# Reordering VectorE and ScalarE around the second projection and attention, the norm behind them and a gated mixer's first chunk

## The reference, cut to what matters

```python
for i in range(2):
    h = h + 0.5 * swiglu(rmsnorm(h, norm_g[i, 0]), ffn_w_in[i, 0], ffn_w_out[i, 0])
    hn = rmsnorm(h, norm_g[i, 1])
    h = h + (mixer_a(hn, ...) if i == 0 else mixer_b(hn, ...))
    h = h + 0.5 * swiglu(rmsnorm(h, norm_g[i, 2]), ffn_w_in[i, 1], ffn_w_out[i, 1])
return rmsnorm(h, final_g)
```

```python
# mixer_a: q, k, v (8 heads of 128), index queries qi (8 x 64), index key ki (64), index weights wi (8)
q, k, v, qi, ki, wi = split(h @ w_in)
rel = relu(einsum('bthd,bsd->bths', qi, ki) * 64 ** -0.5)
score = einsum('bth,bths->bts', wi, rel)                 # masked causally; the top 64 keys of a query stay
logits = q . k * 128 ** -0.5 + bias_by_distance           # the other keys get -inf
out = softmax(logits) @ v @ w_out
# mixer_b: u and v have 3072 columns each; sv is a causal product over 128 positions, for each of 8 groups
u, v = split(gelu(h @ w_in + b_in)); v = layernorm(v)
out = (u * (tril(w_sp[group]) @ v + b_sp[group])) @ w_out
```

## Time and profile before

| what | us |
|---|---|
| median of 3 executions | 1426.86 |
| lowest and highest | 1425.26, 1428.1 |
| profiled execution, its own time | 1428.46 |
| its span, from the first instruction to the end of the last | 1426.7 |
| TensorE busy | 1383.6 |
| VectorE busy | 965.2 |
| ScalarE busy | 676.8 |
| waits of TensorE at the start for the first slab | 13.5 |

### The profile page before, as it was taken

The page is one execution under the profiler, slowest core; times in us unless marked ns, Lnnn a source line. Parts: engine busy times, 40 slices in busy tenths (PEclk is TensorE's granted clock), DMA queues, the critical chain, the costliest instruction groups (busy, mean ns, idle before and its releaser), DMA issues.

```text
span 1426.7 us, 18656 instructions
## 1 busy us (share of the span) xinstructions
PE 1383.6 (97%) x7514; PEld 1192.4 (84%) x7514; DVE 965.2 (68%) x1174; ACT 676.8 (47%) x824; POOL 48.1 (3%) x76
## 2 busy tenths in 40 slices
PE   6999999999999999999999999999999999999997
PEld 5868888888888879877888888888888788888886
DVE  5536766577766667767766667666667777686664
ACT  5432444345444454345545465454553444564542
POOL 1001000001000000002000000000000000000000
PEclk9879999999999999999999999999999999999999
DMA  8612845545555445244555536545374455365540
GB/s 324 213 34 106 304 177 181 204 147 202 198 204 194 181 173 206 86 151 164 207 200 204 184 119 247 196 177 181 137 302 163 170 205 191 134 233 199 204 156 30
DMA packets 37732, 259.91 MB, mean 182 GB/s; under 512 B 4344, under 2 KB 4384, under 8 KB 7696
## 3 DMA queue, kind: packets, MB, share of 16 engines
q1 hardware_dynamic: 34272, 245.38, 46.6%
q0 software_dynamic: 3376, 13.34, 2.7%
HBM read 257.65 MB, written 2.63 MB: 182 GB/s over the span
## 4 chain that ended last, share of the span: by engine, by line
PE 90%; DVE 5%; ACT 2%; DMA 1%; issue 1%; POOL 0%; DVEq 0%; POOLq 0%; SPq 0%; ACTq 0%
PE tp L1362 14%; PE mm L1362 14%; PE acc L1219 10%; PE acc L1221 10%; PE acc L1220 10%; PE tp L1369 7%; PE mm L1369 7%; PE mm L1219 4%; PE mm L1220 4%; PE mm L1221 4%; DVE wlo L735 2%; ACT whi L486 1%; DMA raw<-slabs_dram 1%; PE acc L1674 1%; PE acc L1316 1%
## 5 line engine op out<-in xcount | busy, mean ns | idle before, releaser
L735 DVE TENSOR_TENSOR wlo<-raw,whi 128x2048 fp32r<-128x2048 f32 x232 | 529.1, 2288 | 61.2 <-ACT whi L486 60.8
L486 ACT ACTIVATE whi<-raw 128x2048 fp32r<-128x2048 f32 x232 | 442.0, 1910 | 37.6 <-DMA raw<-slabs_dram 30.4
L1362 PE MATMUL mm<-xt,whi 128*128 128x512 f32 x896 | 234.7, 393 | 1.9 <-DVE xt L808 1.9
L1362 PE MATMUL tp<-xt,whi 128*128 128x512 f32 x896 | 234.0, 392 | 0.0
L1219 PE MATMUL acc<-whi,ht 128*128 128x512 f32 x576 | 227.8, 396 | 2.0 <-DVE ht L848 1.0
L1220 PE MATMUL acc<-wlo,ht 128*128 128x512 f32 x576 | 224.8, 390 | 0.0
L1221 PE MATMUL acc<-whi,ht 128*128 128x512 f32 x576 | 224.8, 390 | 0.0
L1362 PEld LDWEIGHTS mm<-xt,whi 128*128 128x128 f32 x896 | 160.5, 189 | 29.9 <-DVE xt L808 2.3
L1362 PEld LDWEIGHTS tp<-xt,whi 128*128 128x128 f32 x896 | 160.7, 189 | 27.6
L558 ACT ACTIVATE ht<-hid 128x256 fp32r<-128x256 f32 (+1 forms) x116 | 54.4, 469 | 166.1 <-DVE hid L897 123.8
L1369 PEld LDWEIGHTS tp<-xt,wlo 128*128 128x128 f32 x896 | 123.1, 190 | 9.3
(11 more groups left out here) (186 smaller groups left out, 1558.7 us busy)
## 6 DMA issues: line engine op xcount, KB each, us to landing
raw<-slabs_dram SPq DMA_DIRECT2D x232, 1024.0 KB, 4.9
vec<-vectors_dram POOLq DMA_DIRECT2D x12, 512.0 KB, 5.8
tables_dram<-table_dram POOLq DMA_DIRECT2D x1, 1536.0 KB, 9.7
hlf<-x_turned_dram SPq DMA_DIRECT2D x2, 512.0 KB, 7.0
h<-x_dram POOLq DMA_DIRECT2D x2, 512.0 KB, 4.1
htf<-tables_dram POOLq DMA_DIRECT2D x1, 1024.0 KB, 6.1
htf<-vectors_dram POOLq DMA_DIRECT2D x1, 1024.0 KB, 9.2
h<-bands_dram POOLq DMA_DIRECT2D x1, 768.0 KB, 7.6
```

The costliest lines, as they stand in the source:

```text
L486: nc.scalar.activation(whi[:, m % RING, :], raw[:, m % RAW, :], ACT.Copy).then_inc(hi_done, 1)
L735: nc.vector.tensor_tensor(wlo[:, m % RING, :], raw[:, m % RAW, :], whi[:, m % RING, :], ALU.subtract).then_inc(lo_done, 1)
L1362: ins = nc.tensor.matmul(halves_of(out), w[0], xt[:, :, k, :], start=k == 0, stop=k == KD - 1)
```

## The change

The instructions stay as they are; their places in the lists change.

- Second projection: VectorE makes the low part of slab 81 before it copies unit 0, that of slab 82 before unit 1, and holds back one slab part each after units 2 and 3. TensorE makes the first index scores between the two halves (j = 0, 1) of unit 5 and not before it.
- Second attention: ScalarE and VectorE make their parts of slab 93 earlier, ScalarE before the first exponentials. ScalarE turns the first token tile's copies ahead of `exps(2)`. VectorE finds the last maxima before it copies unit 14, and makes the low part of slab 94 behind both. TensorE turns the attention's first tile in the middle of unit 14.
- Norm: VectorE makes the third group's low part before the fourth addition, and ScalarE makes its slab part after the third group.
- Mixer: VectorE normalizes chunk 1 after it takes unit (1,0), and not ahead of unit (0,1). Both engines leave out the slab part at the end of chunk 0, so that it falls to chunk 1. TensorE makes chunk 1's spatial products behind both tiles of the unit.

The diff, cut to what matters:

```diff
@@ ScalarE: norm
                     if g == 1 and n.order is BY_TILE:
                         if squares:
                             square(n, 0)
+                    if g == (2 if n is n3 else 1) and n.order is BY_TILE:
                         splits.upto(min(splits.next + 1, n.split_to))
@@ ScalarE: fused, chunk 0
                         for i in range(2):
                             hidden_hi(0, i)
-                        splits.upto(by)
+                        if stg is not mixb:
+                            splits.upto(by)
@@ ScalarE: attention
+                if a is att2:
+                    splits.upto(end + 1)
                 exps(0)
                 exps(1)
                 splits.upto(end + 1)
...
                 splits.upto(end + 4)
+                if a is att2:
+                    to_xt(0)
                 exps(2)
-                to_xt(0)
+                if a is att1:
+                    to_xt(0)
                 turned(2)
@@ VectorE: norm
                 xt_lo(n, 1)
-                add_acc(n, src, 3, factor, 4, True)
-                xt_lo(n, 2)
+                if n is n3:
+                    xt_lo(n, 2)
+                    add_acc(n, src, 3, factor, 4, True)
+                else:
+                    add_acc(n, src, 3, factor, 4, True)
+                    xt_lo(n, 2)
@@ VectorE: fused
                         splits.upto(split_by(stg, f, 0, 0))
-                        if stg is mixb:
-                            for i in range(2):
-                                normalize_v(1, i)
                         taken(0, 1)
...
                             hidden_lo(0, i)
-                        splits.upto(by)
+                        if stg is not mixb:
+                            splits.upto(by)
...
                         taken(c, i)
+                        if stg is mixb and (c, i) == (1, 0):
+                            normalize_v(1, 0)
+                            normalize_v(1, 1)
@@ VectorE: attention
                 between()
-                splits.upto(end + 2)
                 if a is att1:
+                    splits.upto(end + 2)
                     maxima(2)
...
                 turned(0)
+                maxima(3)
                 filler()
-                maxima(3)
                 splits.upto(end + 4)
@@ VectorE: second projection
             for n, u in enumerate(A_UNITS[:-2]):
+                if n < 2:
+                    splits.upto(u.m + 4 + n)
                 evacuate(a_in, n, u)
-                splits.upto(u.m + (RING if n < LAST_A - 3 else 2))
+                if n > 0:
+                    splits.upto(u.m + (RING - (n in (GATE_UNIT, QI_UNIT - 1)) if n < LAST_A - 3 else 2))
@@ TensorE: project (new argument middle=None)
                     for j in range(2):
+                        if j == 1 and middle is not None:
+                            middle()
@@ TensorE: downs
-                        if stg is mixb and q == 2 * i:
+                        if stg is mixb and q == 2 * i + (c == 0):
                             spatial(c + 1, i)
@@ TensorE: second projection
-                    project(a_in, n, u)
+                    project(a_in, n, u, (lambda: index_scores(0)) if n == QI_UNIT + 1 else None)
...
-                if n in INDEX_AFTER:
+                if n in INDEX_AFTER and n != QI_UNIT:
                     index_scores(INDEX_AFTER[n])
@@ TensorE: v_tile1
-                project(a_in, LAST_A, A_UNITS[LAST_A])
+                pe.wait_ge(a_in.evac, LAST_A - 1)
+                u = A_UNITS[LAST_A]
+                token_part(LAST_A % 2, u.m, u.i, range(4), release=True)
                 turn()
+                token_part(LAST_A % 2, u.m, u.i, range(4, KD), release=True)
```

More of the change, by code:

```diff
@@ L1254, in token_unit, with project @@
                 token_part(bank, m, t, range(KD), None if last else ready, last)
-            def project(stg, n, u):
+            def project(stg, n, u, middle=None):
                 if n >= 2:
```

## The result

| | before | after |
|---|---|---|
| median, us | 1426.84 | 1413.12 |
| lowest and highest, us | 1425.09, 1428.1 | 1411.1, 1413.98 |
| executions | 6 | 6 |
| profiled execution, its own time and span, us | 1428.46, 1426.7 | 1411.4, 1409.7 |

The ratio is 0.9903, with a 95% interval of 0.9891 to 0.9916. In microseconds that is 13.7 less, between 12.0 and 15.5. The forecast was 1412.9.

What follows compares the result with a forecast made beforehand. TensorE, busy 97% of the span, was taken as the bound. Waits 11.1, clock 1.7 and restarts 1.0 made 13.8 us, rounded to 14: 1428.46 to 1414.5, the median 1.6 less, 1412.9; range 1410.5 to 1416.5.

Steps and rivals of the forecast that it cites:

- Second projection: TensorE's waits for VectorE's copies of units 1 and 4 go: 2.3 and 0.8 us gained.
- Second attention: TensorE's waits of 2.1, 1.1 and 1.2 us for value copy, low part and exponential go: 4.4 us.
- Norm: At the norm behind the second attention, the third group's earlier low part gains 0.8 of a 1.9 us wait.
- Mixer: In the mixer's first chunk, waits of 0.9 and 2.5 us go, less a new wait of 0.6 us.
- restarts: On TensorE, each wait that goes gives 0.17 us more; seven go and one comes: 1.0 us.
- the bill: In the mixer, VectorE's unchanged work causes a new spatial-product wait at chunk 2, between 0 and 2.0 us; taken as 0.6.
- Rival B: Waits in the second attention come back in another form, costing 1 to 2.3 us: 1415; chance 0.15.
- Rival A: VectorE becomes the bound in the mixer, new wait 2.0 us and low clock 1.7: time 1416; chance 0.17.
- The clock: In the mixer's first chunk, the 1.2 GHz stretch behind both waits goes with them: 1.7 us gained.
- C: Across the changed stages, most waits only change place: gain under 8 us, about 1421; chance 0.06.
- D: Whole kernel within 0.2% of before, 1427, another releaser standing behind each named wait; chance 0.02.
- E: Slower: in the attention, postponed slab parts make loads late, two waits totalling 18 us, about 1431; chance 0.02.

Runs made afterwards that it cites:

- e9: The changed kernel with ScalarE's exponentials of group 2 ahead of its copies of the turned attention again; 1414.29 us.
- e10: The changed kernel with VectorE's copy of the last value unit ahead of the last maxima again; 1413.95 us.
- e11: The changed kernel with the last value unit in one piece again and the turn of the attention behind it; 1416.73 us.
- e6: The changed kernel with the slab part at the end of the mixer's chunk 0 back on ScalarE and VectorE; 1413.11 us.
- e7: The changed kernel with chunk 1's spatial products back behind the first tile of each unit; 1416.62 us.
- e12: The kernel before, unchanged, run and profiled once more; 1427.49 us.
- e2: The kernel before with the mixer part of the change alone; 1422.87 us.
- e3: The changed kernel with all of the second attention's part put back as before; 1416.69 us.
- e1: The changed kernel with the whole mixer part put back as before; 1416.62 us.
- e4: The changed kernel with the second projection's part put back as before; 1416.07 us.

## Why the prediction was right

**Second projection: right.** Both waits are gone, 3.1 us and two restarts of 0.17 make 3.44, and the stage shows 3.40. VectorE after, in the projection (start, duration, idle time before):

```profile
517.83 0.75 DVE L1035 TENSOR_SCALAR reg<-mm,st 128x512 f32<-128x512 f32 x1 [0.84 <-POOL st L395]
518.78 2.29 DVE L742 TENSOR_TENSOR wlo<-raw,whi 128x2048 fp32r<-128x2048 f32 x1 [0.20 <-ACT whi L486]
520.99 0.74 DVE L1035 TENSOR_SCALAR reg<-mm,st 128x512 f32<-128x512 f32 x1
```

The block of three low parts of the earlier trace rows is now broken up; the copy of unit 1 ends at 521.73. The forecast was 524.4 on the clock of the profile before, whose projection starts 2.6 us later: 521.8.

**Second attention: right, margins too.** Three waits, 4.4 us and 0.5 for their restarts make 4.9; the stage shows 5.13. VectorE after, from the end of the third maxima:

```profile
602.56 1.29 DVE L759 TENSOR_TENSOR xt<-tp,xt 128x512 fp32r<-128x512 f32 x2 [0.57 <-ACT xt L493]
603.77 1.22 DVE L1182 SCALAR_TENSOR_TENSOR acc<-acc,htf 128x1024 f32<-128x1024 f32 x1
...
607.63 0.74 DVE L1035 TENSOR_SCALAR reg<-mm,st 128x512 f32<-128x512 f32 x1
608.29 6.68 DVE L742 TENSOR_TENSOR wlo<-raw,whi 128x2048 fp32r<-128x2048 f32 x3
```

ScalarE after, the last of `exps(2)`, and the end of `exps(3)`:

```profile
604.25 0.49 ACT L615 ACTIVATE hid<-acc,st 128x256 f32<-128x256 f32 x1
604.61 0.23 ACT L615 ACTIVATION_READ_ACCUMULATOR hid<-acc,st 128x1 f32 x1
...
609.47 0.21 ACT L615 ACTIVATION_READ_ACCUMULATOR hid<-acc,st 128x1 f32 x1
```

And TensorE after, at the four places where it could have waited:

```profile
604.93 1.05 PE L1572 MATMUL tp<-idf,hid 128*128 128x128 f32 x8
...
608.59 1.95 PE L1587 MATMUL mm<-reg,hlf 128*128 128x128 f32 x16
610.38 1.04 PE L1572 MATMUL tp<-idf,hid 128*128 128x128 f32 x8
611.17 0.48 PE L1234 MATMUL acc<-whi,xt 128*128 128x512 f32 x1
```

| margin, us | forecast | measured |
|---|---|---|
| `exps(2)` ends ahead of its turn | 0.2 | 604.93 - 604.84 = 0.1 |
| copy of the last unit ahead of the values | 0.3 | 608.59 - 608.37 = 0.2 |
| `exps(3)` ends ahead of its turn | 0.8 | 610.38 - 609.68 = 0.7 |
| low part of slab 94 ahead of the output projection | 0.8 | 0.7 |

The last is the first of the three at 608.29: at 2.2 us apiece it ends near 610.5, and its first use is at 611.17. Rival B was the right one to fear: with margins of 0.1 and 0.2 us, e9, e10 and e11 show that undoing any one of three orders lets a wait of its kind come back, at 1.45 to 2.76 us.

**Norm: right.** 1.9 us became 1.0; 0.8 was forecast and 0.84 measured.

**Mixer: right, in the sum and in the place of the bill.** The spatial product of chunk 1 has no wait. VectorE after:

```profile
1092.34 0.68 DVE L840 TENSOR_TENSOR hid<-tp,hid 128x512 f32<-128x512 f32 x1
...
1095.30 0.75 DVE L948 SCALAR_TENSOR_TENSOR reg<-reg,st,htf 128x512 f32<-128x512 f32 x1
...
1096.64 6.69 DVE L742 TENSOR_TENSOR wlo<-raw,whi 128x2048 fp32r<-128x2048 f32 x3
1103.24 0.69 DVE L927 TENSOR_TENSOR tp<-tp,bspb 128x512 f32<-128x512 f32 x1
...
1107.42 0.68 DVE L840 TENSOR_TENSOR hid<-mm,hid 128x512 f32<-128x512 f32 x1
...
1117.73 0.68 DVE L840 TENSOR_TENSOR hid<-tp,hid 128x512 f32<-128x512 f32 x1
```

It takes (1,0) at 1092.34 and has normalized chunk 1 at 1096.05. TensorE starts the spatial product of (1,0) at 1096.81, so 0.8 us were to spare where the forecast had 1.3. VectorE makes the postponed low parts in one block from 1096.64, which are 6.7 us without idle time. The bill falls on the next units. Before, VectorE was idle for 2.18 us ahead of unit (1,1) and for 1.06 us ahead of (2,0), the first unit of chunk 2 (the forecast read the 1.06 at a later unit, where it is the same):

```profile
1133.87 0.69 DVE L829 TENSOR_TENSOR hid<-tp,hid 128x512 f32<-128x512 f32 x1 [1.06 <-ACT hid L548]
```

After, (1,1) at 1107.42 and (2,0) at 1117.73 have no idle time ahead of them, and TensorE waits for the second:

```profile
1118.56 1.13 PE L1817 MATMUL tp<-reg 128*128 128x128 f32 x8 [0.45 <-DVE hid L840]
```

The bill was forecast as 0.6 between bounds of 0 and 2.0, and is 0.45. The bounds were worked out, the 0.6 was picked between them, so that it came so near is in part luck. VectorE won back more than the 3.2 us that the forecast allowed: the mixer begins 12.23 us earlier than before, and (2,0) is taken 1133.87 - 1117.73 = 16.14 us earlier, 3.9 more. Rival A, with 2.0 there and a low clock, did not come. Waits 0.9 + 2.5 - 0.45, one restart net (0.17) and 1.7 for the clock make 4.8, beside 4.86 measured.

**The clock: the size was right, a reason wrong.** "If a drop needed only one wait of 2 us, the attention would have had it" does not hold. In e6 and e7 one wait of 2.54 and of 1.86 us was enough in the mixer, and in e12 one of 2.3 in the projection; the same 2.3 was not enough in three other profiles, and the 2.1 in the attention, shown in before, e2, e3 and e12, never was, nor was the 2.56 there in e11. The 3.0 of the earlier feed-forward was followed by a low clock in 11 profiles of 14. The three profiles with both mixer waits (before, e1, e12) all have the low clock, and with e6 and e7 it is five of five with a wait of 1.86 us or more at this place. So the forecast gain of 1.7 was there in every pair of profiles that this study can compare, but the forecast took one profile's clock for a property of the size of the waits. What decides whether a given wait brings it stays open; size alone does not. The Trainium skill's rule (the same page, "What's actually happening"), that activity releases the clock, was behind the prediction's warning. The runs agree so far that in the stages of the change the clock fell only behind a wait, and don't show which wait will do it.

**The sum.** 13.8 was forecast against the profiled execution, rounded to 14; the stages show 14.2. That the median came within 0.2 us of the forecast owes something to luck: the forecast took the profile's start-up as the typical one, and medians of the same kernel differ by as much as 1.0 us from one group of runs to another (1426.84 and 1427.84 for the kernel before). Rivals C and D are excluded, since no wait came in the place of the seven but 0.45 us, and E too: no row of the table names a slab part in the attention's output.

**By medians alone** three of the parts would have been misjudged a little: against the kernel after, which was timed in another group of runs, e1 loses 3.5 us by its median and 4.86 by its stage, e3 3.6 and 5.13, e4 3.0 and 3.38. The start-up column of these kernels' profiles is 499.88, 502.79 and 502.50, and it can go either way.

## What to carry to other kernels

Where one engine is busy for 97% of the span, take its table of waits, and for each row ask what stands ahead of the awaited instruction in its engine's list and could stand behind it; the durations in the profile gave the margins of the new order to 0.1 us in the attention and to 0.5 us in the mixer. Moves that belong together have to be made together: the early copies without the cut unit left a wait of 2.56 us where the old order had one of 1.1 at this place. For a part worth 3 us in 1400, compare the starts of the same matmul in two profiles, not the totals.

## What the runs showed of the hardware that was not expected

- The 1.2 GHz stretch came behind a single wait of 1.86 us (e7), and not behind others of 2.1 and 2.56 (attention), nor in three of four cases behind the same one of 2.3 us (projection), nor in three of 14 behind the same one of 3.0 us (earlier feed-forward). The cost was 1.7 us in the mixer and 1.4 in the projection, in addition to the wait.
- The second projection began between 499.4 and 502.8 us over 14 profiles, behind instructions that no kernel here changes. In the pair that was compared, 2 of 2.6 us were lost to more time at 1.2 GHz in the first attention.
- The feed-forward waits for `ht` total 1.3 us in some kernels and 0.7 to 1.0 in others, with the same orders around them; why was not looked into.
